# Second block's attention: gate and softmax scale applied to the probabilities, gated values taken in transposed form

## The reference, cut to what matters

```
gates = sigmoid(g_a).reshape(B, S, 8 heads, 3 branches)
# gated ("NSA") half, 8 heads of 64, 2 key/value groups:
s = q . k * scale;  p = masked_softmax(s)          # once per branch
o_cmp = p_cmp @ v_cmp     # 15 compressed keys
o_sel = p_sel @ v_sel     # causal, up to 256 keys
o_win = p_win @ v_win     # causal, up to 256 keys
o_a = gates[..., 0:1] * o_cmp + gates[..., 1:2] * o_sel + gates[..., 2:3] * o_win
# latent ("MLA") half, 8 heads, 96-wide keys, no gates:
o_b = masked_softmax(q_b . k_b * scale_b) @ v_b
mixed = concatenate([rms_norm(o_a, nsa_out_norm), rms_norm(o_b, mla_out_norm)])
x = x + mixed @ w_out
```

## Time and profile before

| | us |
|---|---|
| median of 3 runs | 2312.87 |
| lowest and highest | 2312.30, 2314.44 |
| the profiled execution | 2314.22 |
| its span | 2312.40 |
| its mean granted clock of TensorE | 0.99 of 2.4 GHz |

### The profile page before, as it was taken

How to read it: one execution, slowest core, us unless ns; L and a number is a source line. 1 busy time by engine, 2 the same in 40 slices (tenths; PEclk the granted TensorE clock), 3 DMA queues, 4 the chain that set the end, 5 groups by cost and what they waited for, 6 DMA issues and landing times.

```text
span 2312.4 us, 25907 instructions
## 1 busy us (share of the span) xinstructions
PE 2184.3 (94%) x9548; PEld 1098.6 (48%) x9548; DVE 971.3 (42%) x1810; ACT 376.6 (16%) x1035; POOL 173.6 (8%) x206
## 2 busy tenths in 40 slices
PE   6989999999999999989999888899899999999998
PEld 2436554333333344455333333335668644668843
DVE  3667433344433457473222222235721345551245
ACT  2006221000000010062111111012511001331100
POOL 0210002000000013131000000000000000000000
PEclk9999999999999999999999999999999999999999
DMA  9783548999999962355999999974234443414442
GB/s 374 258 295 137 217 166 326 420 421 421 421 421 421 421 238 73 69 232 175 419 420 420 421 421 422 421 296 152 86 110 146 146 177 125 171 37 146 146 149 96
DMA packets 153117, 603.03 MB, mean 261 GB/s; under 512 B 15012, under 2 KB 28068, under 8 KB 103488
## 3 DMA queue, kind: packets, MB, share of 16 engines
q1 hardware_dynamic: 145120, 594.74, 66.0%
q0 software_dynamic: 4736, 5.99, 0.8%
q10 hardware_dynamic: 3168, 1.03, 0.2%
HBM read 606.90 MB, written 4.73 MB: 264 GB/s over the span
## 4 chain that ended last, share of the span: by engine, by line
PE 78%; DMA 10%; DVE 8%; issue 2%; ACT 1%; SPq 1%; POOL 1%; DVEq 0%; ACTq 0%; POOLq 0%
PE psum L2942 16%; PE psum L2432 10%; PE psum L3156 10%; DMA ring<-in_w 9%; PE psum L3178 8%; PE psum L2982 7%; PE psum L2952 6%; PE psum L2326 5%; PE psum L3037 4%; PE psum L2574 2%; PE psum L2445 2%; DVE arena L1924 1%; PE psum L2332 1%; PE psum L2654 1%; PE psum L2311 1%
## 5 line engine op out<-in xcount | busy, mean ns | idle before, releaser
L2942 PE MATMUL psum<-arena 128*64 128x512 f32 x616 | 268.9, 595 | 10.4 <-DMA ring<-in_w 9.8
L2942 PE MATMUL psum<-ring,arena 128*64 128x512 f32 x712 | 267.9, 596 | 0.0
L1837 DVE TENSOR_TENSOR X<-X,psum 128x512 f32<-128x512 f32 x192 | 132.0, 688 | 269.9 <-PE psum L2952 269.7
L3156 PE MATMUL psum<-hT,ring 128*128 128x256 f32 x1024 | 224.7, 383 | 2.6 <-DVE hT L1957 2.6
L3156 PEld LDWEIGHTS psum<-hT,ring 128*128 128x128 f32 x1024 | 197.1, 193 | 29.8 <-DVE hT L1957 3.0
L2982 PE MATMUL psum<-extra,arena 128*64 128x512 f32 x432 | 191.0, 596 | 0.0
L2952 PE MATMUL psum<-arena 128*128 128x512 f32 x384 | 178.4, 602 | 0.0
L2432 PE MATMUL psum<-ring,hT 128*128 128x512 f32 x384 | 168.4, 594 | 1.9 <-DVE hT L1596 0.7
L2326 PE MATMUL psum<-con,arena 128*128 128x128 f32 (+1 forms) x832 | 118.5, 282 | 26.4 <-DVE arena L1924 10.2
L2942 PEld LDWEIGHTS psum<-arena 128*64 128x64 f32 x616 | 79.5, 137 | 117.5 <-issue 116.6
L2326 PEld LDWEIGHTS psum<-con,arena 128*128 128x128 f32 (+1 forms) x832 | 92.2, 142 | 82.4 <-issue 24.8
(11 more groups left out here) (409 smaller groups left out, 2990.4 us busy)
## 6 DMA issues: line engine op xcount, KB each, us to landing
ring<-in_w SPq DMA_DIRECT2D x126, 1024.0 KB, 21.5
arena<-in_w SPq DMA_DIRECT2D x84, 1024.0 KB, 19.0
ring<-in_w_ff SPq DMA_DIRECT2D x64, 1024.0 KB, 5.8
extra<-in_w SPq DMA_DIRECT2D x62, 1024.0 KB, 19.6
rows<-in_w SPq DMA_DIRECT2D x49, 1024.0 KB, 18.1
ring<-in_w_mod SPq DMA_DIRECT2D x32, 1024.0 KB, 14.2
gate<-in_w SPq DMA_DIRECT2D x30, 1024.0 KB, 22.9
hT<-in_w SPq DMA_DIRECT2D x18, 1024.0 KB, 16.6
```

The costliest lines, as they stand in the source:

```text
L1837: dve.tensor_tensor(x, x, bank, ALU.add).then_inc(v_free, 1)
L2942: inst = pe.matmul(out[64 * e:64 * e + 64, :], xgT[:, b, k, 64 * e:64 * e + 64], m, start=k == 0, stop=k == KB - 1)
L3156: inst = pe.matmul(bank[:, SEQ * f:SEQ * f + SEQ], w[k][:, at:at + P], hT[:, k, 0:SEQ], start=k == 0, stop=k == KB - 1)
```

## The change

In gated groups VectorE no longer scales the output. `weigh(n)` multiplies the reciprocal of the sums by `keep` and gate as before, and then multiplies the whole of `probs` by it, ahead of the transposes; `turn(n)` waits for that (`att_p`) where it waited for the exponentials. `values` of a gated group uses the values as the weight and the transposed probabilities as the moving operand, so the result has features on the partitions and tokens in the columns, which is the form that `output_T` made. All branches of a tile are summed in PSUM bank 6; VectorE takes the sum once per tile, with the norm's gain (`summed_T`), straight into `hT`. The quarters 0 and 2 of `output_T` go. Since the gated half is no longer in `oA`, ScalarE squares bank 6 in transposed form (`nsa_squares`, after groups 3 and 9) and TensorE sums the squares over the partitions by products with a column of ones (bank 5), at the head of `mixed_output`; ScalarE copies the sums and squares the latent half after that. Scores, maxima and exponentials run two groups ahead instead of one, and `turn(n)` comes before `values(n-1)`.

The diff, cut to its core:

```diff
+            def nsa_squares(l, m):
+                act.wait_ge(o_taken, 4 * l + m + 1)
+                act.activation(rows[:, m, 0:512], psum[:, 6, :], ACT.Square).then_inc(nsa_squared, 1)
             def mix_squares(l):
+                act.wait_ge(mix_sums, l + 1)
+                act.activation(sumsq[:, 1:3, 0], psum[:, 5, 0:2], ACT.Copy)
                 for m in range(2):
-                    for h in range(2):
-                        act.wait_ge(att_o, 11 * l + (4, 4, 9, 11)[2 * m + h])
-                        inst = act.activation(arena[:, 16384 + 1024 * m + 512 * h:16896 + 1024 * m + 512 * h], oA[:, m, 512 * h:512 * h + 512], ACT.Square, accum_out=sumsq[:, 1 + m, h:h + 1])
-                    inst.then_inc(mix_ready, 1)
+                    act.wait_ge(att_o, 3 * l + (1, 3)[m])
+                    act.activation(arena[:, 16384 + 1024 * m:16896 + 1024 * m], oA[:, m, 512:1024], ACT.Square, accum_out=sumsq[:, 1 + m, 1:2]).then_inc(mix_ready, 1)
...
                 exps(groups[0])
+                exps(groups[1])
...
-                    if n + 1 < len(groups):
-                        exps(groups[n + 1])
+                    if n + 2 < len(groups):
+                        exps(groups[n + 2])
+                    if n in (3, 9):
+                        nsa_squares(l, n // 9)
...
+                def weigh(n):
+                    g = groups[n]
+                    b, heads = (11 * l + n) % 4, len(g["heads"])
+                    dve.wait_ge(att_e, 11 * l + n + 1)
+                    r = rden[:, b, 0:heads]
+                    dve.reciprocal(r, psums[:, b, 0:heads]).then_inc(v_step, 1)
...
+                    dve.tensor_tensor(r.rearrange("p (s t) -> p s t", s=2), r.rearrange("p (s t) -> p s t", s=2), chosen_gates, ALU.mult).then_inc(v_step, 1)
+                    dve.wait_ge(v_step, so_far(v_step))
+                    p = probs[:, b % 2, 0:heads * g["nk"]].rearrange("p (u n) -> p u n", u=heads)
+                    dve.tensor_tensor(p, p, r[:, :, None].to_broadcast([P, heads, g["nk"]]), ALU.mult).then_inc(att_p, 1)
...
+                def summed_T(m):
+                    dve.wait_ge(nsa_summed, 2 * l + m + 1)
+                    scaled_T(hT[:, 0:4, P * m:P * m + P], psum[:, 6, :], G_MIX + KB * l).then_inc(o_taken, 1)
...
                 maxima(groups[0])
+                maxima(groups[1])
                 for n in range(len(groups)):
-                    if n + 1 < len(groups):
-                        maxima(groups[n + 1])
+                    if "gate" in groups[n]:
+                        weigh(n)
+                    if n + 2 < len(groups):
+                        maxima(groups[n + 2])
                     evac(groups[n])
                     if n + 1 == len(groups):
-                        for j in range(3):
-                            output_T(l, j)
+                        output_T(l, 1)
                     if n:
-                        output(groups[n - 1])
-                output(groups[-1])
+                        finish(n - 1)
+                finish(len(groups) - 1)
...
             def mixed_output(l):
+                pe.wait_ge(nsa_squared, 2 * l + 2)
+                for m in range(2):
+                    for i in range(4):
+                        inst = pe.matmul(psum[:, 5, m:m + 1], rows[:, m, P * i:P * i + P], co("ones", width=1), start=i == 0, stop=i == 3)
+                inst.then_inc(mix_sums, 1)
...
+                    if g["kv"] is None:
+                        if n:
+                            pe.wait_ge(nsa_squared, 2 * l + 1)
+                        v = g["pv_all"].rearrange("p h n -> p (h n)")
+                        for t in range(4):
+                            pe.matmul(o[:, P * t:P * t + P], v[:, P * t:P * t + P], pT[:, 0:P], start=t == 0, stop=False)
+                        return
+                    nb, last = g["nk"] // P, n in (2, 8)
+                    p4 = pT.rearrange("p (s t b n) -> p s t b n", s=2, b=nb, n=P)
+                    for i, kv in enumerate(g["kv"]):
+                        for b in range(nb):
+                            for s in range(2):
+                                inst = pe.matmul(o[64 * s:64 * s + 64, 256 * kv:256 * kv + 256], g["v"][kv][b], p4[:, s, 2 * i:2 * i + 2, b, :],
+                                                 start=False, stop=last and b == nb - 1 and kv == 1)
...
                 scores(0)
+                scores(1)
                 for n in range(len(groups)):
-                    if n + 1 < len(groups):
-                        scores(n + 1)
+                    if n + 2 < len(groups):
+                        scores(n + 2)
+                    if n + 1 == len(groups):
+                        output_T(l, 1)
+                    turn(n)
                     if n:
                         values(n - 1)
-                    if n + 1 == len(groups):
-                        output_T(l, 0)
-                        output_T(l, 1)
-                    turn(n)
-                output_T(l, 2)
                 values(len(groups) - 1)
```

More of the change, by code:

```diff
@@ L459, in groups_2 @@
                                 scores=[(q[h], half(kC, h)[:, h // 4, :]) for h in parted], pv_all=vBD, parted=True,
-                                gate=(m, 0), keep=co("cmp_keep", at=16 * m, width=1), out=oA[:, m, 0:512], first=True))
+                                gate=(m, 0), keep=co("cmp_keep", at=16 * m, width=1), kv=None))
                 for kind in ("sel", "win", "mla"):
@@ L840, in values_c, with attention @@
                     act.activation(value_m1[p], psum[:, VALUE_BANKS[p][0], :], ACT.Copy).then_inc(value_copied, 1)
-            def attention(groups):
+            def attention(l, groups):
                 def exps(g):
@@ L1422, in output @@
                         dve.wait_ge(v_step, so_far(v_step))
[L1423 to L1443, removed]
@@ new lines, in weigh, with output @@
+                    dve.tensor_tensor(p, p, r[:, :, None].to_broadcast([P, heads, g["nk"]]), ALU.mult).then_inc(att_p, 1)
+                    dve.wait_ge(att_p, so_far(att_p))
+                def output(n):
+                    g = groups[n]
+                    dve.wait_ge(att_pv, valued.next())
+                    dve.wait_ge(att_e, 11 * l + n + 1)
+                    b, heads = (11 * l + n) % 4, len(g["heads"])
+                    dve.reciprocal(rden[:, b, 0:heads], psums[:, b, 0:heads]).then_inc(v_step, 1)
+                    dve.wait_ge(v_step, so_far(v_step))
+                    o = psum[:, 7 - n // 10, 0:HD * heads].rearrange("p (u n) -> p u n", u=heads)
+                    dve.tensor_tensor(g["out"].rearrange("p (u n) -> p u n", u=heads), o,
+                                 rden[:, b, 0:heads, None].to_broadcast([P, heads, HD]), ALU.mult).then_inc(att_o, 1)
+                    dve.wait_ge(att_o, so_far(att_o))
@@ L1445, in attention, with finish @@
+                def summed_T(m):
+                    dve.wait_ge(nsa_summed, 2 * l + m + 1)
+                    scaled_T(hT[:, 0:4, P * m:P * m + P], psum[:, 6, :], G_MIX + KB * l).then_inc(o_taken, 1)
+                def finish(n):
+                    if "gate" not in groups[n]:
+                        output(n)
+                    elif n in (2, 8):
+                        summed_T(n // 8)
                 maxima(groups[0])
+                maxima(groups[1])
                 for n in range(len(groups)):
-                    if n + 1 < len(groups):
-                        maxima(groups[n + 1])
+                    if "gate" in groups[n]:
+                        weigh(n)
+                    if n + 2 < len(groups):
+                        maxima(groups[n + 2])
@@ L2601, in turn @@
                 def turn(n):
-                    pe.wait_ge(att_e, base + n + 1)
+                    if "gate" in groups[n]:
+                        pe.wait_ge(att_p, 8 * l + sum("gate" in g for g in groups[:n]) + 1)
+                    else:
+                        pe.wait_ge(att_e, base + n + 1)
                     if base + n:
@@ L2625, in values @@
-                    inst.then_inc(att_pv, 1)
+                    pT = probsT[:, (base + n) % 2, :]
+                    if "gate" not in g:
+                        if n == 9:
+                            pe.wait_ge(att_o, 3 * l + 1)
+                        if n == 10:
+                            pe.wait_ge(nsa_squared, 2 * l + 2)
+                        o, b = psum[:, 7 - n // 10, :], 0
+                        for u, vs in enumerate(g["pv"]):
+                            for m, vb in enumerate(vs):
+                                inst = pe.matmul(o[:, HD * u:HD * u + HD], pT[:, P * b:P * b + P], vb, start=m == 0, stop=m == len(vs) - 1)
+                                b += 1
+                        inst.then_inc(att_pv, 1)
+                        return
```

44 lines of the change are left out of this document (16 added, 28 removed).

## The result

The changed kernel took 2332.4 us in the median of four runs (2328.92 to 2333.71), the kernel before 2313.65 beside it: ratio 1.0081, 95% interval 1.0069 to 1.0093. The forecast was 2318.9, range 2313.0 to 2324.5. The direction held; the size, +18.7 us where +6.0 was forecast, did not. The same kernel run later beside the experiments (`e5`) took 2326.66, ratio 1.0055 (1.0038 to 1.0072), and its profile spans 2319.5 us instead of 2331.9. The term that the miss turns on varies that much for one and the same program.

What follows compares the result with a forecast made beforehand. VectorE was taken to bound tile 1, with TensorE just behind. Stages of 52.8 + 1.7 = 54.5 us against 51.81 and 52.54, plus 0.65 a layer, gave +3.0 each, +6.0 in all: median 2318.9, range 2313 to 2324.5.

Steps and rivals of the forecast that it cites:

- VectorE's work moves to tile 1.: Tile 1's four gated four-head groups: VectorE's period 4.60 us instead of 4.26, +1.4 us; the saving is in tile 0.
- The order, laid out queue by queue.: Attention stage, two groups ahead: three engines' queues laid out put the first output product at 52.8 us without sums.
- Values in pairs.: Gated value passes on TensorE: 8 instructions of 256 columns, in pairs, take 0.97 us instead of 1.73.
- Rival C: Gated value pairs do not overlap: 1.73 us a pass, +1.6 us a layer, 2322 in all; chance 0.06.
- The sum of squares.: Head of `mixed_output`, on TensorE's path: 16 one-column instructions cost 1.7 us, ends 0.9 and 3.5.
- Rival D: Change works as laid out but column sums cost 0.9 us: 2317.3; low edge of the forecast, together chance 0.55.
- ScalarE's chain hidden.: ScalarE's squares at the stage's end finish before VectorE's first reader, over a microsecond to spare: no added time.
- The half-clock stretch may be longer with TensorE idler. I add 0.65 a layer.: Attention stages: 0.65 us a layer added, the old kernel's layout being 0.6 short; +3.0 a layer, +6.0 in all.
- Rival B: TensorE's idling and one-column products bring half-clock stretches in stage and projection: +2.2 us a layer, 2323.4; chance 0.17.
- the layout of 54.5: Attention stage: 52.8 us plus 1.7 for the sums, against 51.81 and 52.54 before: +2.7 and +2.0.
- a single 4 us window with TensorE busy 2.48 us: Earlier profile, 2028 to 2032: TensorE busy 2.48 of 4 us kept clock 1.00; counted against Rival B.
- Rival A: VectorE's multiplication runs at 0.75 us instead of 1.23, TensorE the bound: not slower, 2313.1; chance 0.22.

Runs made afterwards that it cites:

- e6: Changed kernel with unread 512-column products in TensorE's waits and the column sums moved behind the first output-projection product: 2315.28 us, ratio 1.0006.
- e2: Changed kernel with the column sums moved from the head of `mixed_output` to behind the first output-projection product: 2321.61 us, ratio 1.0038.
- e10: Changed kernel with unread 512-column products (fillers) in TensorE's waits in tile 0 only, none from group 3 on: 2321.43 us, ratio 1.0030.
- e1: Changed kernel with unread 512-column products (fillers) in TensorE's waits through the attention stage, column sums left in place: 2323.02 us, ratio 1.0038.
- e8: Changed kernel, fillers to group 6, ScalarE evacuating both transposed banks of six groups, tile 0's sums before group 6's transposes, tile 1's behind first product: 2310.75 us, ratio 0.9981.
- e4: Kernel before with one more 128x256 VectorE product in each gated four-head group's output, 4 a layer: 2318.29 us, ratio 1.0016.
- e11: Changed kernel with each gated value pass of groups 1, 2 and 5 to 8 issued twice, first into an unread bank: 2325.57 us, ratio 1.0052.
- e7: Kernel before with two unread 512-column products ahead of the first transposing pass, in TensorE's first wait: 2312.61 us, ratio 0.9998.
- e3: Changed kernel without the column sums and ScalarE's wait for them, so results are not the reference's: 2319.07 us, ratio 1.0023.

## Why the prediction was wrong

- *VectorE's work moves to tile 1.* Right: 1.225 us a multiplication, periods of 4.60, stage busy time up by 1.6 us.
- *The order, laid out queue by queue.* Right at full clock: 52.8 forecast to the first product without sums, 52.78 in e6.
- *Values in pairs.* Right: 1.0 us a pass at full clock against 0.97. Rival C falls. The Trainium skill (TensorE: Matmul & The Clock Gate, "Part 3: Packing small matmuls", The mechanism) states that a weight load overlaps a running matmul only where the row groups differ. This trace does not agree: they are the same here, and the pass takes 1.0 us with its eight loads.
- *The sum of squares.* Right at full clock: 1.71 to 1.77 us against 1.7. Rival D falls.
- *ScalarE's chain hidden.* Right: e2's projections are longer by the sums alone.
- *"The half-clock stretch may be longer with TensorE idler. I add 0.65 a layer."* This is the step that failed: the term for the clock. Rival B had the mechanism, with a chance of 0.17 and a price of 2.2 us a layer. Against the layout of 54.5, the stages of the changed kernel lost 4.9 and 6.7 us and the projections' heads 2.7 each: 8.5 us a layer. In e5 it was 2.5, 2.7, 0 and 1.5, 3.4 a layer: one and a half times B's price there, four times in the first profile.
- *Why B was priced too small.* I counted one stretch in the stage and one behind it. There were stretches of 10.2, 3.4, 10.2 and 6.8 us in layer 1, and of 17.1, 3.4, 10.2 and 6.8 in layer 2. At half clock TensorE becomes the bound and VectorE waits for it (8.2 us for scores in layer 2, against 2.9 in the layout). TensorE's own waits do not grow by that: 9.4 us in each stage of the first profile, 11.8 and 10.8 in e5 at the higher clock. Why the falls come back through the stage is therefore not shown. Fillers in tile 0 alone went with fewer of them (e10). In layer 2 the 17.1 us begin at 2012.4, ahead of the first score, so the stage's waits did not start them. I had also read the kernel before too narrowly: its fall in layer 2 lasts 6.8 us, from 2007.3 to 2014.1, of which the window in the earlier trace rows is the middle, and layer 1 has one of 3.4. My evidence against B was a single 4 us window with TensorE busy 2.48 us that kept 1.00. e5 shows what such a window is worth: the same instructions fall in one execution and not in another. The Trainium skill (TensorE: Matmul & The Clock Gate, "HAM oscillation") describes bursts and waits for DMA that bring the throttle back each time. The waits here are for VectorE and ScalarE, 2.5 us at most, so it is not the same case; e1 and e6 agree in so far as filled waits came with less half clock, 20.5 and 6.8 us against 68.3 and 37.5.
- *Rival A* falls with the multiplication at 1.225, though its point stands: with VectorE relieved (e8) stage and projection in the transposed form at full clock are level with the old ones.

What stays open: which property of the work matters, TensorE's idle time or how little the narrow passes fill the array. e4 and e11 point to both (behind the longer wait of 1.8 us the clock fell, though the passes were the long ones; doubled passes restore 1.00 in tile 1), and no run here separates them. Fillers change both at once. What can be said of tile 0: no fall began there, behind the first score, in the eight layers with fillers of the changed kernel (e1, e6, e8, e10) or in the two of e7. In the ten without (changed, e2, e3, e5, e11) nine began there.

## What to carry to other kernels

Lay out the queues at full clock, and then lay them out once more with TensorE at half clock; where a change adds waits to TensorE or shortens its passes, that second time is one end of the range, instead of one stretch more. Here a gated group took 5.7 us so, instead of 4.6. Profile the same kernel more than once before explaining where the clock fell. Shortening TensorE's passes under another engine's bound bought nothing here and went with a lower clock (e11). A few wide products in the first waits are a cheap trial: with six a layer (e10) the half clock was 23.9 us, against 68.3 and 37.5 without.

## What the runs showed of the hardware

- The place of a fall changes between executions of one program: stages of 59.42 and 61.20 in one profile, 57.00 and 57.22 in another, with the same instructions in them.
- A one-column product with a full 128x128 weight took 0.107 us, 1.71 for 16 instructions; the profile shows their 16 weight loads back to back over the same stretch (e2). Where the 16 stood behind 64-column passes, with the gated passes not doubled, the head of the projection fell to half clock in 7 of 8 profiled layers (changed, e1, e5, e10); where they (in e8 half of them) stood behind the first 512-column product, in none of six (e2, e6, e8), and without them (e3) in none of two.
- ScalarE evacuates two neighbouring PSUM banks in one instruction of 1.02 us, where one bank takes it 0.60:

```profile
2034.12 1.02 ACT L874 ACTIVATE arena<-psum 128x1024 f32<-128x1024 f32 x1 [2.27 <-PE psum L2357]
```
